# The first stage of a two-block transformer kernel: two channel pairs multiply the un-normalised input, and one product sums the squares

## The chip, the cores and the metric

The kernel runs on one core of a Trainium2 chip. The metric is the time of one execution on the device, in microseconds; of several runs the median is given. The engines of the core run side by side and wait for each other by semaphores: TensorE (PE, with its weight loads PEld), VectorE (DVE), ScalarE (ACT), GpSimd (POOL), and SyncE (SP), which only issues the loads here.

## The reference

Two transformer blocks follow each other on 512 tokens of width 1024, in float32. Only the start of the first one matters here:

```python
def rms_norm(x, g):
    xf = x.astype(jnp.float32)
    y = xf * lax.rsqrt(jnp.mean(xf * xf, axis=-1, keepdims=True) + EPS)
    return (y * g.astype(jnp.float32)).astype(x.dtype)
...
    h = rms_norm(x, norm1_g)
    z = h @ w_in
    q, k, v, xr, yr, gate_logits = jnp.split(z, IN_SPLITS, axis=-1)
...
    rnn = rg_lru(causal_depthwise_conv(xr, conv_w, conv_b), w_rg_a, b_rg_a, w_rg_x, b_rg_x,
                 rg_lambda) * jax.nn.gelu(yr)
```

xr and yr have 1280 columns each. The factor 1/sqrt(mean) depends on the token alone, so it can be applied to a column of `h @ w_in` after the product as well as before it. Attention, merge, an expert layer and the whole second block follow.

## The kernel before

**Tiles.** The activations stand transposed, channels on partitions, 512 tokens in the free dimension: X is eight tiles of 128x512. A weight unit is 128 output columns: 128x1024, that is eight blocks of 128x128 for the eight k. Each float32 operand is cut into a high and a low part, and a product is three matmuls (lines 719 to 721, `triple`). ScalarE makes a weight's high part (line 1277), VectorE its low part (line 1748). `raw` holds five loaded units and `whl` five cut ones.

**Order of the units.** `unit_order()` fixes it: 0 and 1 are w_in 24 and 34 (xr and yr of channel pair 0), 2 and 3 pair 1, 4 and 5 pair 2, 6 and 7 pair 3, then two gate units and small ones. Each engine's program is written out by hand and walks through this list; `weights(name, i)` means: cut (or load) up to NW - 1 = 4 units past this one. An engine works strictly in its program's order, so a cut waits for what is written before it.

**The first stage.** SP loads the parameters, X in four quarters, the constants `cst`, five weight units and the lambdas. ScalarE squares each X[k] into scr[k] and forms the high part of X[k] times its gain, VectorE the low part (`gained`). TensorE first sums the squares over the channels with eight products with a matrix of ones (`sums`, line 754), then multiplies pair 0 with the un-normalised, gained X (`two`). ScalarE turns the sum into the factor r (Ln and Exp, which need a function table), VectorE scales X to H (`norm`: one product, line 1756, and one difference, line 1748, per k), ScalarE makes H's high part in between. Pair 0's products are scaled by r out of PSUM by VectorE in `conv4(0)`: xr into `pad`, yr into ST. From pair 1 on TensorE multiplies H, and ScalarE copies xr from PSUM to `pad`.

**Around the change.** Per pair VectorE runs `conv4` (one product, three chained steps), ScalarE the conv's high part, then gelu of yr, with a function table of its own, and between them stand the cuts of later weights. After pair 1's conv VectorE runs `scalars()`, a chain of some thirty small instructions with two exponentials of ScalarE in it; the low part of unit 7 follows behind it. In names of tiles, `whl` is a cut weight, `pb` PSUM, `S` and `ST` one memory under two types.

Of the kernel before, what the change touches and what calls it, by code (L numbers as in the profile page):

```python
# [491 lines left out]
def build(nc, a, out):  # L492
    with ExitStack() as ctx:
# [119 lines left out]
        gh, gl, first_q = oh, ol, (sum_sq, one_sq)  # L613
        o_root = [scr[8]] * 7 + [scr[7]]
# [100 lines left out]
        def tensor(eng, e):  # L715
# [17 lines left out]
            def two(j, outs, hh, hl, ready, done, tag=None):  # L733

                for k in range(8):
                    if k == 4 and tag:
                        sum_of(tag)
# [8 lines left out]
            def sum_of(tag):  # L746
                q.wait_ge(pool, ("sq", tag))
                e.matmul(bank[7], ones, sum_sq, start=True, stop=True, skip_group_check=True).then_inc(
                    prod.up(("sums", tag)), 1)

            def sums(tag, sq, b, lhs=ones):
                for k, s in enumerate(sq):
                    q.wait_ge(act, ("sq", tag, k))
                    last = e.matmul(b, lhs, s, start=k == 0, stop=k == len(sq) - 1, skip_group_check=True)
                last.then_inc(prod.up(("sums", tag)), 1)
# [30 lines left out]
            def recurrence():  # L786
                q.wait_ge(cst_in, "cst")
                sums("1", scr[0:8], bank[7])
                for c in range(0, 10, 2):
                    for d in (c, c + 1):  # L790
                        i = d % 2
                        if d == 0:
                            j = q.unit("w_in", 24)
                            q.unit("w_in", 34)
                            two(j, (bank[0], bank[2]), gh, gl, [("g", "1", k) for k in range(8)], (("xr", 0), ("yr", 0)))
                            continue
                        if d == 2:
                            q.wait_ge(dve, "xr_scaled")
                        elif d > 2:
# [460 lines left out]
        def scalar(eng, e):  # L1260
            q, hi_done, logs = Waits(eng, units), [0], [False]
# [89 lines left out]
            def recurrence():  # L1351
                q.wait_ge(prm_in, "prm")
                for k in range(8):
                    q.wait_ge(x_in[k // 2], ("x", k // 2))
                    run(ACT.Square, scr[k], X[k]).then_inc(act.up(("sq", "1", k)), 1)
                    e.activation(gh[k], X[k], ACT.Copy, scale=prm("norm1_g", k)).then_inc(act.up(("ghi", "1", k)), 1)
                    if k == 5:
                        split(2)
                norm("1", scr, scr[8], bank[7], Hh, lambda: split(4))
                for c in range(0, 10, 2):  # L1360
                    for d in (c, c + 1):
# [4 lines left out]
                        if d:  # L1366
# [1413 lines left out]
```

## Time and profile before

| | us |
|---|---|
| median of 3 runs | 2969.61 (2969.41 to 2971.81) |
| profiled execution, its own time | 2972.36 |
| span of the profiled execution, first to last instruction | 2970.2 |
| TensorE busy | 2921.5 (98%) |
| VectorE busy | 1906.8 (64%) |
| ScalarE busy | 1152.3 (39%) |
| GpSimd busy | 842.9 (28%) |

The profile shows one execution; its own time is 2.2 us more than its span. Matmuls overlap, so a busy TensorE is not one at its peak. Of the chain that ended last 80% lies on TensorE, 12% on VectorE and 4% on ScalarE, and the first stage is the first 60 to 90 us of it. In the rows further down L719 to L721 are the three matmuls of a product.

### The profile page before, as it was taken

The page shows a single profiled execution, that of the slowest core. Times are in us where ns is not written, and L with a number is a line of the kernel's source. Part 1 is how long each engine was busy: PE and PEld are TensorE (multiplying, and loading weights), DVE is VectorE, ACT ScalarE, POOL GpSimd, SP SyncE. Part 2 cuts the span into 40 slices and gives each one's busy share as a digit, 9 for nine tenths or more (in the row PEclk, how much of TensorE's full clock was granted, in tenths as well). Part 3 has the DMA queues.
Part 4 walks back from the last instruction along what each step waited for, and adds up shares of the span by engine and source line. Part 5 has one row for each costly group of instructions (what it writes and reads, how often), then busy time and mean ns, then how long its engine had stood idle before and what let it go on. Part 6 is the DMA issues. An engine that isn't in the chain of part 4 may idle for free.

```text
span 2970.2 us, 35823 instructions
## 1 busy us (share of the span) xinstructions
PE 2921.5 (98%) x14079; PEld 2509.6 (84%) x14079; DVE 1906.8 (64%) x3255; ACT 1152.3 (39%) x1704; POOL 842.9 (28%) x523
## 2 busy tenths in 40 slices
PE   8999999999999999999999999999999999999999
PEld 6877777789889999999999999998888877788887
DVE  6664665578888895426787788865444567644443
ACT  5674665443333334433323223223222355532221
POOL 0000000228788888872332232321000400210000
PEclk9999999999999999999999999999999999999999
DMA  4325564336656666798988888842332321133222
GB/s 141 112 92 212 199 223 167 132 103 144 136 127 139 153 154 146 166 272 322 333 311 308 287 310 314 318 142 86 99 100 94 122 71 50 51 99 99 93 93 71
DMA packets 240808, 489.29 MB, mean 165 GB/s; under 512 B 97664, under 2 KB 149440, under 8 KB 240128
## 3 DMA queue, kind: packets, MB, share of 16 engines
q1 hardware_dynamic: 175680, 417.87, 42.3%
q0 software_dynamic: 64960, 69.14, 10.3%
q8 instruction: 111, 1.82, 0.2%
q14 instruction: 57, 0.47, 0.0%
HBM read 443.18 MB, written 77.23 MB: 175 GB/s over the span
## 4 chain that ended last, share of the span: by engine, by line
PE 80%; DVE 12%; ACT 4%; issue 3%; POOL 1%; DMA 0%; SPq 0%; POOLq 0%; ACTq 0%
PE pb L719 25%; PE pb L721 25%; PE pb L720 25%; DVE whl L1748 2%; ACT scr L1274 2%; DVE ST L1748 1%; ACT whl L1277 1%; PE pb L1011 1%; DVE ST L1756 1%; DVE S L1748 1%; DVE su L1997 1%; DVE ST L1998 1%; DVE su L2000 1%; DVE scr L1748 1%; PE pb L894 1%
## 5 line engine op out<-in xcount | busy, mean ns | idle before, releaser
L719 PE MATMUL pb<-H,whl 128*128 128x512 f32 (+1 forms) x2400 | 939.7, 392 | 6.4 <-ACT scr L1274 2.3
L721 PE MATMUL pb<-H,whl 128*128 128x512 f32 (+1 forms) x2400 | 911.5, 380 | 0.0
L720 PE MATMUL pb<-H,whl 128*128 128x512 f32 (+1 forms) x2400 | 910.8, 380 | 0.0
L1748 DVE TENSOR_TENSOR whl<-raw,whl 128x1024 fp32r<-128x1024 f32 (+5 forms) x554 | 650.7, 1189 | 256.3 <-ACT whl L1277 219.8
L1277 ACT ACTIVATE whl<-raw 128x1024 fp32r<-128x1024 f32 (+5 forms) x554 | 544.6, 1003 | 361.2 <-PE pb L721 360.1
L719 PE MATMUL pb<-S,whl 128*128 128x448 f32 (+2 forms) x1732 | 654.9, 378 | 14.2 <-DVE S L1748 5.7
L720 PE MATMUL pb<-S,whl 128*128 128x448 f32 (+2 forms) x1732 | 649.6, 375 | 0.0
L721 PE MATMUL pb<-S,whl 128*128 128x448 f32 (+2 forms) x1732 | 649.5, 375 | 0.0
L719 PEld LDWEIGHTS pb<-H,whl 128*128 128x128 f32 x2400 | 451.4, 188 | 83.8 <-issue 8.8
L720 PEld LDWEIGHTS pb<-H,whl 128*128 128x128 f32 x2400 | 451.5, 188 | 72.2 <-issue 6.0
L721 PEld LDWEIGHTS pb<-H,whl 128*128 128x128 f32 x2400 | 450.6, 188 | 71.9
L2400 POOL DMA_INDIRECT gd<-scr,place x256 | 438.2, 1712 | 137.8 <-issue 77.1
L719 PEld LDWEIGHTS pb<-S,whl 128*128 128x128 f32 x1732 | 327.9, 189 | 60.9 <-DVE S L1748 7.2
L720 PEld LDWEIGHTS pb<-S,whl 128*128 128x128 f32 x1732 | 327.8, 189 | 42.6 <-issue 1.2
L721 PEld LDWEIGHTS pb<-S,whl 128*128 128x128 f32 x1732 | 327.6, 189 | 42.5
L2379 POOL TENSOR_TENSOR pad<-X 128x512 f32<-128x512 f32 x32 | 46.2, 1442 | 862.4 <-DVE X L1748 833.3
L1274 ACT ACTIVATE scr<-pb 128x448 f32<-128x448 f32 (+1 forms) x130 | 71.0, 546 | 386.2 <-PE pb L721 364.5
L1748 DVE TENSOR_TENSOR scr<-pb,scr 128x512 f32<-128x512 f32 x96 | 66.0, 691 | 210.7 <-PE pb L721 199.7
L2433 POOL DMA_INDIRECT scr<-in_pv_rows,su x64 | 94.8, 1482 | 232.1 <-DVE scr L1756 204.8
L1277 ACT ACTIVATE S<-GA 128x896 fp32r<-128x896 f32 x60 | 57.2, 953 | 252.6 <-DVE GA L1748 247.0
L2387 POOL DMA_INDIRECT scr<-in_pu_rows,su x64 | 91.8, 1434 | 217.0 <-DVE scr L1756 167.0
L1748 DVE TENSOR_TENSOR X<-X,pb 128x448 f32<-128x448 f32 (+1 forms) x144 | 86.2, 630 | 92.8 <-PE pb L721 78.8
(224 smaller groups left out, 2573.8 us busy)
## 6 DMA issues: line engine op xcount, KB each, us to landing
raw<-in_pu SPq DMA_DIRECT2D x128, 512.0 KB
raw<-in_pv SPq DMA_DIRECT2D x128, 512.0 KB
raw<-in_w_in SPq DMA_DIRECT2D x72, 512.0 KB
ad<-scr SPq DMA_DIRECT2D x128, 224.0 KB
GA<-gd SPq DMA_DIRECT2D x60, 448.0 KB, 4.2
GA<-ad SPq DMA_DIRECT2D x60, 448.0 KB, 5.9
raw<-in_wg SPq DMA_DIRECT2D x44, 512.0 KB
raw<-in_wu SPq DMA_DIRECT2D x44, 512.0 KB
```

Of the source, the lines that this page charges most:

```text
L719: e.matmul(o, lh, h, start=start, stop=False, skip_group_check=True)
L720: e.matmul(o, lh, l, start=False, stop=False, skip_group_check=True)
L721: return e.matmul(o, ll, h, start=False, stop=stop, skip_group_check=True)
L894: e.matmul(b[:, 0:keys], x[r, t], y[r, 0:keys], start=start, stop=False, skip_group_check=True)
L1011: last = e.matmul(bank[gbank[n % 4]][:, c], hot2[n % 4][:, c], hot1[n % 4][:, c], start=True, stop=True, skip_group_check=True)
L1274: return e.activation(o, x, func, **kw)
L1277: return e.activation(o, x, ACT.Copy)
L1748: return e.tensor_tensor(o, x, y, op)
L2379: e.tensor_tensor(one_sq if k else sum_sq, x, x, ALU.mult).then_inc(pool.up(), 1)
L2387: e.indirect_dma_start(urow[j % 3] if j < UROWS else tail_row[j % 4], None, a["pu_rows"], bass.IndirectOffsetOnAxis(ap=expert[:, j:j + 1], ...
L2400: e.indirect_dma_start(g_rows, bass.IndirectOffsetOnAxis(ap=place[:, b, h, k:k + 1], axis=0), TSv[:, b, h, k:k + 1], None, compute_op=ALU. ...
L2433: e.indirect_dma_start(tail_row[j % 4], None, a["pv_rows"], bass.IndirectOffsetOnAxis(ap=expert[:, j:j + 1], axis=0)).then_inc(row_in[j % ...
```

## The change

Pair 1 now multiplies the un-normalised X as pair 0 does, and both of its results are scaled by VectorE. For that the parts of the gained X stand elsewhere (g1h, g1l), so that ST's pieces for yr 0 and 1 stay free. The squares are added on VectorE into scr[0], and TensorE forms one sum product in place of eight, inside pair 1 before its second k (`at_k=1`). ScalarE loads the function table for Ln and Exp as its first instruction. SP loads units 0 and 1 right behind X's first quarter. The cuts of units 0 to 4, the constants' work of VectorE and the scaling of xr 0 are moved in the order.

```diff
@@ -611,6 +611,7 @@
 gh, gl, first_q = oh, ol, (sum_sq, one_sq)
+g1h, g1l = cut(S_t[:, 1024:5120], 8), cut(S_t[:, 6144:10240], 8)
 o_root = [scr[8]] * 7 + [scr[7]]
@@ -730,10 +731,10 @@
-    def two(j, outs, hh, hl, ready, done, tag=None):
+    def two(j, outs, hh, hl, ready, done, tag=None, at_k=4):
...
         for k in range(8):
-            if k == 4 and tag:
+            if k == at_k and tag:
                 sum_of(tag)
@@ -744,15 +745,13 @@
     def sum_of(tag):
-        q.wait_ge(pool, ("sq", tag))
-        e.matmul(bank[7], ones, sum_sq, start=True, stop=True, skip_group_check=True).then_inc(
+        if tag == "1":
+            q.wait_ge(cst_in, "cst")
+            q.wait_ge(dve, "sq_sum")
+        else:
+            q.wait_ge(pool, ("sq", tag))
+        e.matmul(bank[7], ones, scr[0] if tag == "1" else sum_sq, start=True, stop=True, skip_group_check=True).then_inc(
             prod.up(("sums", tag)), 1)
-
-    def sums(tag, sq, b, lhs=ones):
-        for k, s in enumerate(sq):
-            q.wait_ge(act, ("sq", tag, k))
-            last = e.matmul(b, lhs, s, start=k == 0, stop=k == len(sq) - 1, skip_group_check=True)
-        last.then_inc(prod.up(("sums", tag)), 1)
@@ -784,19 +783,18 @@
     def recurrence():
-        q.wait_ge(cst_in, "cst")
-        sums("1", scr[0:8], bank[7])
+        g1 = [("g", "1", k) for k in range(8)]
         for c in range(0, 10, 2):
...
                 i = d % 2
-                if d == 0:
-                    j = q.unit("w_in", 24)
-                    q.unit("w_in", 34)
-                    two(j, (bank[0], bank[2]), gh, gl, [("g", "1", k) for k in range(8)], (("xr", 0), ("yr", 0)))
+                if d < 2:
+                    j = q.unit("w_in", 24 + d)
+                    q.unit("w_in", 34 + d)
+                    two(j, (bank[i], bank[2 + i]), g1h, g1l, g1, (("xr", d), ("yr", d)), "1" if d else None, 1)
                     continue
-                if d == 2:
-                    q.wait_ge(dve, "xr_scaled")
-                elif d > 2:
+                if d < 4:
+                    q.wait_ge(dve, ("xr_scaled", d - 2))
+                else:
                     q.wait_ge(act, ("xr_raw", d - 2))
@@ -1258,7 +1256,8 @@
 def scalar(eng, e):
-    q, hi_done, logs = Waits(eng, units), [0], [False]
+    q, hi_done, logs = Waits(eng, units), [0], [True]
+    e.preload_act_table_set("natural_log_exp_and_others")
@@ -1350,22 +1349,28 @@
         q.wait_ge(prm_in, "prm")
-        for k in range(8):
-            q.wait_ge(x_in[k // 2], ("x", k // 2))
-            run(ACT.Square, scr[k], X[k]).then_inc(act.up(("sq", "1", k)), 1)
-            e.activation(gh[k], X[k], ACT.Copy, scale=prm("norm1_g", k)).then_inc(act.up(("ghi", "1", k)), 1)
+        for k in range(10):
+            if k < 8:
+                q.wait_ge(x_in[k // 2], ("x", k // 2))
+                e.activation(g1h[k], X[k], ACT.Copy, scale=prm("norm1_g", k)).then_inc(act.up(("ghi", "1", k)), 1)
+            if k == 1:
+                split(2)
+            elif k > 1:
+                run(ACT.Square, scr[k - 2], X[k - 2]).then_inc(act.up(("sq", "1", k - 2)), 1)
             if k == 5:
-                split(2)
-        norm("1", scr, scr[8], bank[7], Hh, lambda: split(4))
+                split(3)
+            elif k == 7:
+                split(4)
+        norm("1", scr, scr[8], bank[7], Hh, lambda: split(5))
         for c in range(0, 10, 2):
...
                     weights("w_in", 34)
-                if d:
+                if d > 1:
                     q.wait_ge(prod, ("xr", d))
-                    q.wait_ge(dve, ("conv", d - 2) if d > 1 else ("pad0", i))
+                    q.wait_ge(dve, ("conv", d - 2))
                     copy(pad[i][:, 32:544], bank[i]).then_inc(act.up(("xr_raw", d)), 1)
@@ -1380,11 +1385,11 @@
                     run(ACT.Exp, sq[1], sq[1]).then_inc(act.up("softplus_exp"), 1)
-                if d:
+                if d > 1:
                     q.wait_ge(prod, ("yr", d))
                 else:
-                    q.wait_ge(dve, "yr_scaled")
-                run(ACT.Gelu_apprx_tanh, rlf[d], bank[2 + i] if d else rlf[0]).then_inc(act.up(("gelu", d)), 1)
+                    q.wait_ge(dve, ("yr_scaled", d))
+                run(ACT.Gelu_apprx_tanh, rlf[d], bank[2 + i] if d > 1 else rlf[d]).then_inc(act.up(("gelu", d)), 1)
             if c:
@@ -1770,9 +1775,10 @@
-    def norm(tag, xs, gains, sq, r, hi, lo, mid=lambda: None):
+    def norm(tag, xs, gains, sq, r, hi, lo, mid=lambda: None, between=lambda k: None):
         mid()
         for k in range(9):
+            between(k)
             if k < 8:
@@ -1810,15 +1816,20 @@
+    def scaled_x(c):
+        q.wait_ge(prod, ("xr", c))
+        tt(pad[c][:, 32:544], bank[c], scr[8], ALU.mult).then_inc(dve.up(("xr_scaled", c)), 1)
+
     def conv4(c, beside=()):
         i, cv, w = c % 2, rhf[c], [prm("conv_w", 4 * c + j) for j in range(4)]
-        if c:
+        if c > 1:
             q.wait_ge(act, ("xr_raw", c))
         else:
-            q.wait_ge(prod, ("xr", 0))
-            then(tt(pad[0][:, 32:544], bank[0], scr[8], ALU.mult), "xr_scaled")
-            q.wait_ge(prod, ("yr", 0))
-            tt(rlf[0], bank[2], scr[8], ALU.mult).then_inc(dve.up("yr_scaled"), 1)
+            if c:
+                scaled_x(1)
+            q.wait_ge(prod, ("yr", c))
+            tt(rlf[c], bank[2 + c], scr[8], ALU.mult).then_inc(dve.up(("yr_scaled", c)), 1)
+            q.wait_ge(dve, dve.n)
         then(ts(cv, pad[i][:, 32:544], w[3], ALU.mult, prm("conv_b", c), ALU.add))
@@ -1853,10 +1864,17 @@
         q.wait_ge(prm_in, "prm")
-        for k in range(8):
-            gained("1", k, "norm1_g", gh, gl, ("g", "1", k))
-            if k == 5:
+        for k in range(10):
+            if k < 8:
+                gained("1", k, "norm1_g", g1h, g1l, ("g", "1", k))
+            if k == 1:
                 split(2)
+            elif k == 8:
+                split(4)
+            if k > 2:
+                q.wait_ge(act, ("sq", "1", k - 2))
+                then(tt(scr[0], scr[0], scr[k - 2], ALU.add), *(["sq_sum"] if k == 9 else []))
+        norm("1", X, gains("norm1_g"), scr, scr[8], Hh, Hl, between=lambda k: scaled_x(0) if k == 2 else split(5) if k == 4 else None)
         q.wait_ge(cst_in, "cst")
@@ -1865,7 +1883,6 @@
             e.memset(pad[i][:, 0:32], 0.0).then_inc(dve.up(("pad0", i)), 1)
-        norm("1", X, gains("norm1_g"), scr, scr[8], Hh, Hl, lambda: split(4))
         for c in range(0, 10, 2):
@@ -2455,8 +2472,8 @@
-    def load_x(name):
-        for i in range(4):
+    def load_x(name, quarters=range(4)):
+        for i in quarters:
             e.dma_start(X_t[:, 1024 * i:1024 * i + 1024].rearrange("p (k t) -> p k t", k=2),
@@ -2472,7 +2489,9 @@
         e.dma_start(prm_t[:, :], a["prm"]).then_inc(prm_in.up("prm"), 16)
-        load_x("x")
+        load_x("x", (0,))
+        load(2)
+        load_x("x", (1, 2, 3))
         e.dma_start(cst_t[:, :], a["cst"]).then_inc(cst_in.up("cst"), 16)
@@ -2490,6 +2509,7 @@
         q.wait_ge(dve, ("h", "1", 7))
+        q.wait_ge(dve, ("yr_scaled", 1))
         q.wait_ge(dve, "lambda_sums")
...
         load_gate(1, 9, 1)

```

What stands on TensorE at its start before (scr are the squares, L754 the sum products, then pair 0):

```order
L754 MATMUL pb<-scr,cst 128x512 [waits act_results,constants_landed]
L754 MATMUL pb<-scr,cst 128x512 [waits act_results] x7
L719 MATMUL pb<-S,whl 128x512 [waits weight_low_parts,dve_results]
L720 MATMUL pb<-S,whl 128x512
L721 MATMUL pb<-S,whl 128x512
L719 MATMUL pb<-S,whl 128x512 [waits weight_low_parts]
L720 MATMUL pb<-S,whl 128x512
```

TensorE with the change, from the end of pair 0 to the second k of pair 1 (L753 is the sum product):

```order
L720 MATMUL pb<-S,whl 128x512
L721 MATMUL pb<-S,whl 128x512
L722 MATMUL pb<-S,whl 128x512
L720 MATMUL pb<-S,whl 128x512 [waits weight_low_parts]
L721 MATMUL pb<-S,whl 128x512
L722 MATMUL pb<-S,whl 128x512
L720 MATMUL pb<-S,whl 128x512 [waits weight_low_parts]
L721 MATMUL pb<-S,whl 128x512
L722 MATMUL pb<-S,whl 128x512
L753 MATMUL pb<-scr,cst 128x512 [waits dve_results,constants_landed]
L720 MATMUL pb<-S,whl 128x512
L721 MATMUL pb<-S,whl 128x512
```

The eight sum products ahead of pair 0 are gone; one stands behind all of pair 0 and the first k of pair 1.

VectorE before, at the end of the norm and the start of pair 0's conv (unit 4's low part, the two scalings, the conv):

```order
L1756 SCALAR_TENSOR_TENSOR scr<-X,prm,scr 128x512
L1748 TENSOR_TENSOR H<-scr,H 128x512 [waits act_results] x2
L1748 TENSOR_TENSOR whl<-raw,whl 128x1024 [waits weight_high_parts]
L1748 TENSOR_TENSOR pad<-pb,scr 128x512 [waits pe_products]
L1748 TENSOR_TENSOR ST<-pb,scr 128x512 [waits pe_products,dve_results]
L1753 TENSOR_SCALAR ST<-pad,prm 128x512
L1756 SCALAR_TENSOR_TENSOR ST<-pad,prm,ST 128x512 [waits dve_results] x3
```

VectorE with the change, from the norm's first product on:

```order
L1761 SCALAR_TENSOR_TENSOR scr<-X,prm,scr 128x512 [waits act_results,dve_results]
L1761 SCALAR_TENSOR_TENSOR scr<-X,prm,scr 128x512
L1753 TENSOR_TENSOR H<-scr,H 128x512 [waits act_results]
L1753 TENSOR_TENSOR pad<-pb,scr 128x512 [waits pe_products]
L1761 SCALAR_TENSOR_TENSOR scr<-X,prm,scr 128x512
L1753 TENSOR_TENSOR H<-scr,H 128x512 [waits act_results]
L1761 SCALAR_TENSOR_TENSOR scr<-X,prm,scr 128x512
L1753 TENSOR_TENSOR H<-scr,H 128x512 [waits act_results]
L1753 TENSOR_TENSOR whl<-raw,whl 128x1024 [waits weight_high_parts]
L1761 SCALAR_TENSOR_TENSOR scr<-X,prm,scr 128x512
```

The scaling of xr 0 and the low part of unit 4, which stood behind the norm, now stand within it, ahead of its third and fifth product.

ScalarE from H's high parts to the high part of unit 5 (the `whl<-raw` of weights_landed0), before:

```order
L1277 ACTIVATE H<-scr 128x512 [waits dve_results] x8
L1277 ACTIVATE whl<-raw 128x1024 [waits weights_landed4]
L1277 ACTIVATE S<-ST 128x512 [waits dve_results]
L1274 ACT_TABLE_LOAD
L1274 ACTIVATE ST<-ST 128x512
L1277 ACTIVATE whl<-raw 128x1024 [waits pe_products,weights_landed0]
L1277 ACTIVATE pad<-pb 128x512 [waits pe_products]
```

ScalarE with the change, from the high part of unit 4 to that of unit 5:

```order
L1276 ACTIVATE whl<-raw 128x1024 [waits weights_landed4]
L1273 ACTIVATE scr<-pb,cst 128x512 [waits pe_products]
L1273 ACTIVATE scr<-scr 128x512 [waits act_results]
L1276 ACTIVATE H<-scr 128x512 [waits dve_results] x8
L1276 ACTIVATE S<-ST 128x512 [waits dve_results]
L1273 ACT_TABLE_LOAD
L1273 ACTIVATE ST<-ST 128x512
L1276 ACTIVATE whl<-raw 128x1024 [waits weights_landed0]
```

Unit 4 now stands ahead of the norm, unit 5 as before behind the conv's high part, the table load and gelu(0), and the copy to `pad` is gone.

## Rows read from the trace of the kernel before

**Rows 1.** The chain that ended last, its start: start us, us, what.
```profile
3.07 7.91 DMA cst<-in_cst
11.02 10.04 PE pb L754 x16
21.08 1.28 ACT L1267
...
40.59 1.28 ACT L1274
...
42.52 0.96 ACT whl L1277
...
58.62 1.14 DVE whl L1748
```

**Rows 2.** Timeline of TensorE: start us, us, engine line op, operands, xcount, [idle before <-releaser].
```profile
20.49 0.79 PE L719 MATMUL pb<-S,whl 128*128 128x512 f32 x1
...
31.81 0.39 PE L719 MATMUL pb<-H,whl 128*128 128x512 f32 x1
...
59.89 0.47 PE L719 MATMUL pb<-H,whl 128*128 128x512 f32 x1 [0.71 <-DVE whl L1748]
```

**Rows 3.** Busy us (xcount) by stretch: stretch, length, PE, PEld, DVE, ACT, POOL, PEclk, DMA share, GB/s.
```profile
60.00:147.00 87.00, 87.00 (x383) 71.77 (x384) 57.67 (x75) 57.50 (x80) 0.00 (x0) 1.00 0.35 117
...
2573.50:2580.30 6.80, 5.15 (x12) 4.09 (x13) 2.97 (x5) 3.58 (x6) 2.38 (x3) 0.50 0.00 0
177.30:180.70 3.40, 3.22 (x8) 2.58 (x9) 1.36 (x3) 3.37 (x6) 0.00 (x0) 0.50 0.51 104
```

**Rows 4.** Timeline of TensorE's weight loads in the eight sum products.
```profile
15.45 0.34 PEld L754 LDWEIGHTS pb<-scr,cst 128*128 128x128 f32 x1 [0.52 <-issue]
16.31 0.34 PEld L754 LDWEIGHTS pb<-scr,cst 128*128 128x128 f32 x1 [0.52 <-issue]
17.03 0.19 PEld L754 LDWEIGHTS pb<-scr,cst 128*128 128x128 f32 x1 [0.38 <-ACT S L1356]
17.46 0.19 PEld L754 LDWEIGHTS pb<-scr,cst 128*128 128x128 f32 x1 [0.24 <-issue]
```

**Rows 5.** DMA issues of 1.1 to 1.5 us, of 1.5 to 2.0, and SP's timeline: us to landing last.
```profile
X<-in_x SPq DMA_DIRECT2D x1, 512.0 KB, 4.2
...
X<-in_x SPq DMA_DIRECT2D x2, 512.0 KB, 4.8
...
1.18 1.84 SPq L2460 DMA_DIRECT2D X<-in_x  x4
```

**Rows 6.** Timeline of ScalarE, high parts.
```profile
7.25 0.71 ACT L1356 ACTIVATE S<-X,prm 128x512 fp32r<-128x512 f32 x1
...
13.52 1.99 ACT L1277 ACTIVATE whl<-raw 128x1024 fp32r<-128x1024 f32 x2
...
17.68 1.99 ACT L1277 ACTIVATE whl<-raw 128x1024 fp32r<-128x1024 f32 x2
```

**Rows 7.** Timeline of VectorE, first stage.
```profile
8.08 0.75 DVE L1756 SCALAR_TENSOR_TENSOR S<-X,prm,S 128x512 fp32r<-128x512 f32 x1 [8.08 <-ACT S L1356]
...
18.48 0.29 DVE L1752 TENSOR_SCALAR prm<-prm 128x1 f32<-128x1 f32 x3
...
19.19 2.32 DVE L1748 TENSOR_TENSOR whl<-raw,whl 128x1024 fp32r<-128x1024 f32 x2
...
32.80 1.48 DVE L1748 TENSOR_TENSOR H<-scr,H 128x512 fp32r<-128x512 f32 x2
...
36.40 0.69 DVE L1748 TENSOR_TENSOR ST<-pb,scr 128x512 f32<-128x512 f32 x1
...
43.50 1.22 DVE L1748 TENSOR_TENSOR whl<-raw,whl 128x1024 fp32r<-128x1024 f32 x1 [2.20 <-ACT whl L1277]
```

**Rows 8.** Timeline of TensorE at two later idle times.
```profile
177.48 0.77 PE L719 MATMUL pb<-S,whl 128*128 128x512 f32 x1 [2.85 <-DVE whl L1748]
...
2575.15 0.80 PE L719 MATMUL pb<-S,whl 128*128 128x512 f32 x1 [2.03 <-DVE S L1748]
```

## What I predict, and from what

> **What bounds the kernel now.** I read first the chain that ended last, from its start, because the change touches only the first stage. It runs [rows 1]: SP issues the loads, the constants `cst` come down (3.07 + 7.91 = 10.98 us), TensorE does the eight sum products from 11.02 for 10.04 us, ScalarE loads a function table at 21.08, the norm follows, and then the chain does *not* go over TensorE. It goes over VectorE and ScalarE: a table load and gelu(0) (40.59 to 42.52), the high part of a weight (42.52), two convolutions, the small chain `scalars()`, and the low part of weight unit 7 (58.62 + 1.14 = 59.76). Only at 59.89 does TensorE take the chain over, after 0.71 us idle [rows 2]. From there it has no idle time up to 147 us [rows 3]. So TensorE's products between 20.49 and 59.2 us are not on the path: what counts is **when the low part of unit 7 is ready**, because whatever shifts it shifts the rest. Units are numbered as they are consumed: 0 and 1 are pair 0 (w_in 24, 34), 2 and 3 are pair 1, 4 and 5 channel pair 2, 6 and 7 channel pair 3.
>
> The second thing to see is TensorE's clock. In the weight loads of the sum products the starts are 0.86 us apart at 15.45 and 16.31, 0.72 at 17.03 and 0.43 at 17.46 [rows 4]. The same operation runs at half rate (1.2 GHz) first and then at full rate (2.4 GHz). The page's granted clock prints 1.00 for all of it, so the pitch decides. A product of the triple takes (31.81 - 20.49) / 48 = 0.236 us at full rate [rows 2].
>
> **Loads.** X's first quarter lands at 1.18 + 4.2 = 5.4 us. The median of the first two is 4.8, so the second, issued 0.46 later, took 5.4 and landed near 7.05; cst, three slots on, landed at 11.0, so a slot takes some 1.4 us [rows 1, 5]. The weights behind it had landed when ScalarE came for them (13.52 and 17.68, without idle time) [rows 6]. The new order keeps the bytes and swaps slots: units 0 and 1 land near 7.05 and 8.5, X's other quarters near 9.7, 11.0 and 12.3, cst near 13.5, units 2 to 4 near 14.8, 16.2 and 17.5.
>
> **Start of the products.** ScalarE's high part takes 1.0 us (two in 1.99) and the high part of one 512-column piece of the gained X 0.71 [rows 6]; VectorE's low part of a weight takes 1.2 [rows 7]. Unit 0: 7.05 + 1.0 + 0.1 + 1.2 = 9.4, so the first product starts near 9.5 instead of 20.49. The table now loads under the wait for X and costs nothing there.
>
> TensorE comes out of idleness, and now the products pay for it, not the sum products. In the trace half rate lasted from 11.02 to between 16.31 and 17.03, that is some 5.8 us [rows 1, 4]. The same length from 9.5 costs 2.9 us. Pair 0 ends at 9.5 + 48 x 0.236 + 2.9 = 23.7. VectorE feeds it: each k needs one 0.75 us piece (8.08) and one add, priced as the 0.69 us of the same shape at 36.40 [rows 7], about 1.45; k = 7 is ready near 19.0, needed near 22. The adds end near 23.4, because the low parts of units 2 and 3 stand between them. Neither is late.
>
> **The sum.** It now stands behind 54 products (at_k = 1 of pair 1). TensorE gets to it at 23.7 + 1.4 = 25.1; two passes at 0.43 and 0.56 from the last issue to the end (20.49 to 21.06 before) make 26.5 [rows 1, 2]. That is **+5.4 us**. Seven sum products are gone, worth 8.8 us on TensorE, but the one left waits behind 15.
>
> **From the sum to unit 7**, by the same rows:
> - the table load of 1.28 at 21.08 is gone [rows 1]: **-1.3**.
> - in the norm VectorE never idles; the change puts scaled_x(0) (0.6) and the low part of unit 4 (1.15) between, takes 34.28 to 36.40 (that low part and the pad scaling, 2.1) away behind h(7), and puts the constants' work of 18.48 to 19.19 (0.7) there instead [rows 7]: 0.6 + 1.15 - 2.1 + 0.7 = **+0.35**.
> - conv 1 started as soon as unit 5's low part (43.50) was through, from a `pad` that ScalarE had copied [rows 7]. Now VectorE scales both banks itself first, 0.6 + 0.7, not hidden since ScalarE waits for this conv: **+1.2**.
> - gelu(0), its table load, and the `scalars()` chain stay as they are: 0.
>
> Sum: 5.4 - 1.3 + 0.35 + 1.2 = **+5.6**. Unit 7 is ready at 59.76 + 5.6 = 65.4, unit 6 near 56.0, unit 5 at 44.72 + 4.4 = 49.1 (the 1.2 comes after it).
>
> **What TensorE does meanwhile.** Pair 1 ends at 23.7 + 11.3 + 0.9 = 35.9 (before: 42.7, so 6.8 ahead). xr(2) uses H, whose last part comes near 39.9, just in time, and ends at 41.5. There unit 5 is missing, because its high part is queued on ScalarE behind the conv and gelu(0), and TensorE stands until 49.2. The lead is gone here: before, yr(2) began at 20.49 + 5 x 5.5 = 48. It idles again for some 2.5 to 3.5 us before unit 7.
>
> **The clock after a wait.** Idle times of 2.85 and 2.03 us in the trace each came with a stretch at clock 0.50, 3.4 and 6.8 us long [rows 3, 8], while 0.71 us before 59.89 did not [rows 2, 3]. The first of these stretches holds eight products in 3.2 us [rows 3]. That costs 1.7 us, or up to 3.4 when it starts in the idle time and lasts. The same is to be expected at 41.5, where it is covered by the next wait, and before unit 7, where nothing covers it, since TensorE is the chain from there: **+1.7**, bounds 0 and 2.9.
>
> Total **+7.2**. The profiled execution would be 2972.36 + 7.2 = 2979.6 (span 2970.2 + 7.2); it was 2.7 above the median of the runs, so the forecast is 2969.6 + 7.2 = **2976.8 us**.
>
> The Trainium skill ("TensorE: Matmul & The Clock Gate", Part 1, on the clock gate) says that where the first rise falls differs from run to run of one kernel and warns against fitting it to a count. The one trace can't show that. [...]
>
> **Bounds of the uncertain terms.** First half-rate stretch: 0 to 3.4 us of loss instead of 2.9 (so -2.9 to +0.5). Second: 0 to 2.9 instead of 1.7. The order of the landings: a slot more or less, -0.3 to +1.4. VectorE's adds are 1.7 us ahead of TensorE; if they take 0.3 us more each (each waits for the one before it to be complete; the two differences from 32.80 take 1.48), they become the last to come and add up to 0.5.
>
> **Rivals.**
> 1. *No clock loss at the second wait, or an early first rise* (within 0.2%). The shift is 5.6, or 7.2 - 2.9 = 4.3: 2974 to 2975.2. For it: two of the terms depend on when the clock changes. Against: the trace's idle times of this size come with the fall.
> 2. *Faster.* If unit 5 and 7 were not late, TensorE's 6.8 us lead at 35.9 would go through to the end: 2969.6 - 6.8 = 2962.8. It decides at 41.5 us: unit 5's low part must be ready by then, and by 52.4 unit 7's. For it: the products do start 11 us earlier and TensorE is busy throughout the trace from 20.49 on. Against: the chain of the trace doesn't touch those products, and ScalarE's row order has unit 5 behind gelu(0). A part of it could be true if the sum came far earlier than 26.5, but it can't issue before 9.5 + 54 x 0.236 = 22.2.
> 3. *The adds or the loads come late* (slower still). If cst or units 2 and 3 land a slot or two late, or the adds pass 25.1 us, everything moves on: +9 to +11, 2979 to 2981.
> 4. *The change does not do what it says*: the order shows that it does; no chance of its own.
>
> **How the numbers follow.** A difference under 0.2% (5.9 us) is about what a measurement of this kernel can't tell from none. Forecast (shift over 5.9 to 9): 0.51, its own range 2975.6 to 2978.7. Rival 1: 0.34. Rival 2: 0.07, with part of a gain (under 0.2%) counted in rival 1. Rival 3: 0.08. So slower 0.51 + 0.08 = 0.59, same 0.34, faster 0.07. The range 2972.0 to 2980.0 leaves out rival 2, the small end of rival 1 and most of rival 3.
>
> **What would show it.** In the profile after: first product near 9.5 us; one sum product, ending near 26.5; VectorE's first norm product near 27.9; TensorE idle about 7.5 us from 41.5, releaser the low part of a weight; again 2 to 4 us ending near 65.4; then no idle time; a clock of 0.50 for some us after each. Wrong would be: no idle time over 2 us between 35 and 66 (rival 2), the sum's end before 23 us (rise early), or a clock of 1.00 right after 65.4 (rival 1).

## The result, and the profile after

| | before | after |
|---|---|---|
| median of 14 runs each, us | 2971.02 (2969.06 to 2973.25) | 2977.96 (2974.39 to 2980.67) |
| profiled execution, span, us | 2970.2 | 2972.6 |
| TensorE busy, us | 2921.5 | 2915.5 |

The changed kernel is slower. Its median is 6.9 us above that of before; the ratio of the two is put at 1.0020, with an interval of 1.0013 to 1.0027, that is 5.9 us (3.9 to 8.0). The forecast was 7.2 us more than before, 2976.8 against a measured 2977.96. The profiled execution of after took 2974.39 us, the shortest of its fourteen.

**The chain that ended last, after** (start us, us, what), to hold beside [rows 1]:

```profile
8.95 0.76 PE pb L720
...
22.98 0.87 PE pb L753 x2
...
42.50 1.28 ACT L1273
...
44.42 0.95 ACT whl L1276
...
52.42 1.23 DVE whl L1753
...
61.83 1.14 DVE whl L1753
```

TensorE is on it at the start, in the first 54 products (8.95 to 22.98) and the one sum product (0.87 us). Then the chain goes over VectorE and ScalarE as before, through the table load of gelu(0) (42.50) and the cuts of units 5, 6 and 7, to the low part of unit 7 at 61.83 + 1.14 = 62.97 (58.62 + 1.14 before).

**TensorE's timeline, after**, to hold beside [rows 2]: its first product, the sum product, and the two waits for a low part:

```profile
8.95 0.76 PE L720 MATMUL pb<-S,whl 128*128 128x512 f32 x1 [8.95 <-DVE whl L1753]
...
22.81 1.02 PE L753 MATMUL pb<-scr,cst 128*128 128x512 f32 x2
...
46.77 0.76 PE L720 MATMUL pb<-H,whl 128*128 128x512 f32 x1 [7.93 <-DVE whl L1753]
...
63.11 0.54 PE L720 MATMUL pb<-H,whl 128*128 128x512 f32 x1 [3.63 <-DVE whl L1753]
```

The first product came 11.5 us earlier (8.95 against 20.49) and pair 1 was done 9.5 us earlier (the next unit starts at 33.24 against 42.69), and all of that was waited away before unit 5 (7.93 us) and again before unit 7 (3.63 us). Unit 7 is used 3.22 us later than before (63.11 against 59.89). Behind it stands what [rows 3] shows of other idle times, a stretch at half rate:

```profile
9.00:12.20 3.20, 3.20 (x8) 2.32 (x9) 3.05 (x4) 3.09 (x6) 0.00 (x0) 1.00 1.01 411
12.20:22.80 10.60, 10.60 (x48) 8.77 (x47) 9.22 (x13) 7.82 (x12) 0.00 (x0) 1.00 0.77 301
...
46.70:49.70 3.00, 2.93 (x7) 2.38 (x8) 2.89 (x5) 0.00 (x0) 0.00 (x0) 0.50 0.15 44
...
63.30:66.80 3.50, 3.50 (x9) 2.71 (x9) 2.70 (x5) 0.99 (x2) 0.00 (x0) 0.51 0.40 150
66.80:150.00 83.20, 83.20 (x368) 68.86 (x367) 54.41 (x70) 55.45 (x78) 0.00 (x0) 1.00 0.35 110
```

These are stretches of after in the columns of [rows 3], PEclk third from the end. In 9:12.2 the page prints 1.00, but eight products in 3.2 us are the half-rate pitch; 48 follow in 10.6. At 46.7 and at 63.3 the clock reads 0.50 (1.2 GHz), at 66.8 it is back at 1.00 (2.4 GHz), and TensorE has no idle time up to 150.

**A mark inside the execution.** TensorE's products behind unit 7 are the same in every kernel here, and one idle time of 2.85 us recurs among them, at 177.48 before [rows 8]. After:

```profile
182.09 0.47 PE L720 MATMUL pb<-S,whl 128*128 128x512 f32 x1 [2.85 <-DVE whl L1753]
```

The part behind this mark takes 2792.7 us before and 2790.5 after, and between 2789 and 2799 in all twelve profiles of this study, with no order that follows the first stage. (The part is the span less the start of the mark.) A profile of one execution therefore says more at the mark than at its end: here + 4.61 us at the mark, + 2.4 at the end.

### The profile page after: what moved, and what is told of

Read it like the earlier page. It is cut to its first block, busy times and chain, and to the rows that moved or that the text cites. A ratio compares the mean times of both kernels' runs of the same rounds, so it can differ in the third digit from the quotient of the medians.

```text
span 2972.6 us, 35808 instructions
## 1 busy us (share of the span) xinstructions
PE 2915.5 (98%) x14065; PEld 2508.2 (84%) x14065; DVE 1913.0 (64%) x3264; ACT 1151.1 (39%) x1702; POOL 844.0 (28%) x523
## 4 chain that ended last, share of the span: by engine, by line
PE 78%; DVE 12%; ACT 4%; POOL 3%; issue 2%; DMA 1%; SPq 0%; POOLq 0%; ACTq 0%; DVEq 0%
PE pb L720 25%; PE pb L722 25%; PE pb L721 25%; DVE whl L1753 2%; POOL gd L2417 2%; ACT scr L1273 1%; ACT whl L1276 1%; DVE su L2014 1%; DVE ST L2015 1%; DVE ST L1753 1%; DVE su L2017 1%; DVE S L1753 1%; DVE ST L1761 1%; PE pb L1009 1%; DVE scr L1753 1%
## 5 line engine op out<-in xcount | busy, mean ns | idle before, releaser
L720 PEld LDWEIGHTS pb<-S,whl 128*128 128x128 f32 x1748 | 330.2, 189 | 70.6 <-issue 11.1
```

The costliest lines, as they stand in the source:

```text
L720: e.matmul(o, lh, h, start=start, stop=False, skip_group_check=True)
```

## The experiments

Each is an edit of one of the two kernels. Runs of one comparison shared a chip; medians of different comparisons are not set against each other, ratios to before are.

### The changed kernel again

> The changed kernel, unchanged, a second time beside the others. Theory (unit 7's readiness plus a half-rate stretch sets the time): 5 to 9 us slower than before. The first product's start (8.95 us in the first profile), the first half-rate stretch (3.2 us there) and the two idle times (7.9 and 3.6 us) are fixed by the program except for the half-rate stretches, which should differ by up to 3 us between executions; that would be the spread of its runs. Rival (nothing varies at the start): the start of the product with unit 7 is at 63.1 us again to within 0.2 us.

Measured: 1.0020 times before (1.0011 to 1.0029). The same rows of TensorE's timeline, the mark last:

```profile
9.21 0.77 PE L720 MATMUL pb<-S,whl 128*128 128x512 f32 x1 [9.21 <-DVE whl L1753]
...
23.89 1.02 PE L753 MATMUL pb<-scr,cst 128*128 128x512 f32 x2
...
47.84 0.77 PE L720 MATMUL pb<-H,whl 128*128 128x512 f32 x1 [7.93 <-DVE whl L1753]
...
64.16 0.47 PE L720 MATMUL pb<-H,whl 128*128 128x512 f32 x1 [3.46 <-DVE whl L1753]
...
183.14 0.47 PE L720 MATMUL pb<-S,whl 128*128 128x512 f32 x1 [2.85 <-DVE whl L1753]
```

The program is the same and so are its two idle times (7.93 and 7.93, 3.63 and 3.46), but the sum product stands at 23.89 in place of 22.81 and unit 7 at 64.16 in place of 63.11. The first product was 0.26 us later, because X's first quarter landed later (ScalarE's first piece starts at 5.53 against 5.20); the rest is the clock: in the nine profiles of kernels that begin with products, the half-rate pitch lasted between 3.2 and 6.3 us. So the rival, that the start is fixed to 0.2 us, fell. The Trainium skill ("TensorE: Matmul & The Clock Gate", Part 1, on the clock gate) says that this point differs from run to run of one kernel; these traces agree (3.2 and 4.7 us in two executions of one program).

### The cut of unit 7 ahead of scalars()

```diff
                         if d == 1:
+                            split(8)
                             scalars()
```

(and the same line on ScalarE ahead of its two exponentials)

> The changed kernel with one more cut of weights (unit 7) written ahead of scalars() on ScalarE and VectorE. Theory: unit 7 is then ready near 55 us, before TensorE wants it at 59.4, so the idle time of 3.6 us before it and the half-rate stretch behind it (1.7 us) go: 5 us less than the changed kernel, so within 0.1% of before. Rival A (the 7.9 us at 38.8 are what costs): about no difference to the changed kernel. Rival B (VectorE is simply 1.2 us later with everything else, scalars() is needed): the idle time comes back before unit 8.

Measured: 1.0022 (1.0013 to 1.0031), no gain. TensorE's timeline:

```profile
47.98 0.76 PE L720 MATMUL pb<-H,whl 128*128 128x512 f32 x1 [7.92 <-DVE whl L1754]
...
61.20 0.50 PE L720 MATMUL pb<-H,whl 128*128 128x512 f32 x1 [0.25 <-ACT ST L1273]
...
69.92 0.80 PE L720 MATMUL pb<-H,whl 128*128 128x512 f32 x1 [2.97 <-DVE whl L1754]
```

The first wait is there as before (7.92), unit 7 no longer waits for its low part, but 2.97 us of idle time stand at 69.92, before unit 8, whose cut is still behind scalars(), with a half-rate stretch behind them: unit 8 takes 8.3 us (69.92 to 78.22) where a unit at full rate takes 5.44. I had expected 5 us less; the rival B of this run is what happened. One cut taken past a chain of 8 us moves the wait by one unit.

### Products into the idle time before unit 7

```diff
+                        if d == 3:
+                            for k in range(5):
+                                triple(bank[5], Hh[k][:, 0:128], Hl[k][:, 0:128], Hh[k], Hl[k], True, True)
                         linear(q.unit("w_in", 34 + d), bank[2 + i], Hh, Hl, h1, ("yr", d))
```

> The changed kernel with 15 added products on TensorE (H with itself into a bank that nobody reads) between xr(3) and yr(3), some 3.4 us of work in the idle time before unit 7. Nothing else is moved. Theory: unit 7 is used at the same time (63.1 in the first profile), but TensorE's clock stays at 1.00 behind it, so the run is 1.7 us (1 to 2.9) faster than the changed kernel. Rival (the idle time alone costs, the clock does not matter): 0 to 0.3 us slower than the changed kernel.

Measured: 1.0011 (1.0002 to 1.0020), median 2976.78 beside 2978.51 of the changed kernel on the same chip, so 1.7 us less; the intervals of the two ratios overlap. Its timeline, with the first of the added products (no `whl` among its operands), unit 7's first and the mark:

```profile
62.05 0.39 PE L720 MATMUL pb<-H 128*128 128x512 f32 x1
...
65.45 0.39 PE L720 MATMUL pb<-H,whl 128*128 128x512 f32 x1
...
182.86 0.49 PE L720 MATMUL pb<-S,whl 128*128 128x512 f32 x1 [2.86 <-DVE whl L1756]
```

And the stretch of 58 to 66 us, in the columns of [rows 3], without a gap and at clock 1.00:

```profile
58.00:66.00 8.00, 8.00 (x37) 6.64 (x36) 6.75 (x31) 3.57 (x6) 0.00 (x0) 1.00 0.00 1
```

The medians alone would not settle it. From the start of unit 7's product to the mark it takes 182.86 - 65.45 = 117.41 us here, 118.98 in both profiles of the changed kernel (182.09 - 63.11, 183.14 - 64.16) and 117.59 before (177.48 - 59.89). Work that computes nothing made this part of the kernel 1.6 us shorter (1.4 if one takes off the 0.15 us by which it delayed unit 7, counted from the sum product): the half-rate stretch is a cost of its own. Its full size shows against the three kernels below in which TensorE does not wait for unit 7 at all: they take 117.24 or 117.25 us to the mark, 1.7 less. The kernel before, with its short wait, itself paid 0.3 of that.

### The cuts moved forward

```diff
-                norm("1", scr, scr[8], bank[7], Hh, lambda: split(5))
+                norm("1", scr, scr[8], bank[7], Hh, lambda: split(7))
+                split(8)
...
-                norm("1", X, gains("norm1_g"), scr, scr[8], Hh, Hl, between=lambda k: scaled_x(0) if k == 2 else split(5) if k == 4 else None)
+                split(7)
+                norm("1", X, gains("norm1_g"), scr, scr[8], Hh, Hl, between=lambda k: scaled_x(0) if k == 2 else None)
+                split(8)
...
                         if d == 1:
+                            split(10)
                             scalars()
...
-                        if d > 1:
+                        if d > 3:
                             q.wait_ge(act, ("gelu", d - 2))
+                        else:
+                            q.wait_ge(dve, ("yr_scaled", d - 2))
```

(The first hunk and a second `split(10)` are ScalarE's, the next two VectorE's, the last TensorE's; in the file they stand in another order.)

> The changed kernel with the cuts moved: units 5 and 6 ahead of the norm (in VectorE's 2.9 us of idle time at 22.5), unit 7 right behind the norm, units 8 and 9 ahead of scalars(); and TensorE's yr(2) and yr(3) wait for the scaling of yr(0) and yr(1) out of PSUM, not for gelu. Theory (TensorE's lead was lost only to late cuts): no idle time over 1 us between 35 and 67 us, unit 7 used near 51 us in place of 63.1, the first gate unit near 56 in place of 65.5 before; 7 to 10 us faster than before, 13 to 17 faster than the changed kernel. Rival (VectorE's chain as a whole, scalars() in it, is the bound of the stage): the idle time only moves to a later unit, and the time is that of before within 2 us.

Measured: 0.9991 (0.9982 to 1.0000), median 2969.11 beside 2972.56, where 7 to 10 us of gain were expected. Its sum product and TensorE's two waits in the timeline:

```profile
23.99 1.10 PE L753 MATMUL pb<-scr,cst 128*128 128x512 f32 x2 [0.32 <-DVE scr L1757]
...
41.23 0.50 PE L720 MATMUL pb<-H,whl 128*128 128x512 f32 x1 [1.14 <-DVE ST L1757]
...
73.15 0.76 PE L720 MATMUL pb<-S,whl 128*128 128x512 f32 x1 [4.39 <-ACT scr L1275]
```

Two stretches of it, in the columns of [rows 3]:

```profile
41.30:68.70 27.40, 27.40 (x120) 22.37 (x120) 21.55 (x55) 10.78 (x15) 0.00 (x0) 1.00 0.15 57
69.00:78.00 9.00, 4.85 (x12) 3.88 (x13) 4.84 (x7) 8.66 (x13) 0.00 (x0) 0.62 0.61 177
```

The 7.93 us are gone: 27.4 us of products without a gap behind 41.3, and unit 7 is used at 52.28 (near 51 expected, 59.89 before). But where before had no wait at all, one of 4.39 us ends at 73.15, for a sigmoid of ScalarE, with a mean clock of 0.62 about it. ScalarE is late because the conv of pair 2 stands behind scalars() on VectorE (the next run tests this), and gelu and the sigmoid behind that conv. The run bundles three things, the cuts, their places on both engines and TensorE's wait for the scaling in place of gelu; "Unit 5 cut in the norm" below shows why a cut alone does not do it. So half of my theory fell: late cuts lost the lead first, scalars() would have lost most of it anyway.

### The cuts moved forward, and scalars() moved to pair 3

```diff
                         if d == 1:
                             split(10)
+                        if d == 3:
                             scalars()
```

(on top of the last edit, and the exponentials on ScalarE likewise)

> The kernel with the early cuts (e4) and scalars(), with its two exponentials on ScalarE, moved from pair 1 to pair 3. In e4 TensorE ran from 41.2 to 68.8 us without idle time and then waited 4.4 us for a sigmoid of ScalarE, which the chain leads back to scalars(); behind it stood a half-rate stretch of 6.8 us (3.4 lost). Theory (scalars() is the last thing on the path of this stage): the wait and the stretch go, so 7 to 8 us less than e4 and 9 to 12 less than before, some 2961. Rival (the sum of VectorE's work bounds the stage): the wait comes back within 10 us behind, and the time stays within 2 us of e4.

Measured: **0.9973 (0.9962 to 0.9984)**, median 2968.17 beside 2975.72 on that chip: 7.6 us faster than before, and so, by the two ratios to before, some 14 faster than the changed kernel. That is less than the 9 to 12 expected. The rival wanted the time within 2 us of the last run; the mark is 5.4 us earlier (171.01 against 176.37). The 7 to 8 expected there took the whole stretch of 6.8 us at half rate as running time, 3.4 lost, but it began at 71.0, inside the idle time, and TensorE ran only from 73.15 to 77.8 in it, which costs 2.3. So 4.4 + 2.3 less the 1.6 us of the wait that is left make 5.1.

TensorE's timeline, the mark last:

```profile
9.37 0.77 PE L720 MATMUL pb<-S,whl 128*128 128x512 f32 x1 [9.37 <-DVE whl L1758]
...
40.71 0.50 PE L720 MATMUL pb<-H,whl 128*128 128x512 f32 x1 [0.36 <-DVE ST L1758]
...
69.83 0.47 PE L720 MATMUL pb<-S,whl 128*128 128x512 f32 x1 [1.62 <-ACT scr L1275]
...
171.01 0.47 PE L720 MATMUL pb<-S,whl 128*128 128x512 f32 x1 [2.85 <-DVE whl L1758]
```

The stretch behind it, in the columns of [rows 3]:

```profile
70.00:150.00 80.00, 80.00 (x353) 66.03 (x353) 54.47 (x71) 58.84 (x82) 0.00 (x0) 1.00 0.36 117
```

The waits are down to 0.36 and 1.62 us, neither with a half-rate stretch behind it, and the mark is at 171.01, 6.5 us ahead of before and 11.1 ahead of the changed kernel. The two pairs' early products pay once nothing on the other two engines is late for what follows. The same moves without the early products could not give this: before, TensorE has no idle time from 20.49 to the mark but the one ahead of unit 7, and the run "Two single edits of the kernel before" below finds 1.2 us to be had there.

### scalars() alone moved to pair 3

```diff
-                        if d == 1:
+                        if d == 3:
                             scalars()
```

(an edit of the changed kernel, the exponentials on ScalarE likewise)

> The changed kernel with nothing but scalars() (and its exponentials) moved from pair 1 to pair 3; units 5 and 6 stay late. Theory: the idle time of 7.9 us before unit 5 stays, the one of 3.6 before unit 7 goes and none replaces it (unit 8's cut no longer stands behind scalars()), with its half-rate stretch of 1.7 us: 5 us less than the changed kernel, within 0.1% of before. Rival (the 7.9 us set the time alone, with the lead): no difference to the changed kernel.

Measured: 0.9994 (0.9985 to 1.0003) beside 1.0020 of the changed kernel in its two comparisons.

TensorE's timeline:

```profile
48.09 0.77 PE L720 MATMUL pb<-H,whl 128*128 128x512 f32 x1 [7.93 <-DVE whl L1753]
...
61.06 0.39 PE L720 MATMUL pb<-H,whl 128*128 128x512 f32 x1
...
178.30 0.48 PE L720 MATMUL pb<-S,whl 128*128 128x512 f32 x1 [2.84 <-DVE whl L1753]
```

The stretch behind it, in the columns of [rows 3]:

```profile
58.00:150.00 92.00, 92.00 (x408) 76.17 (x407) 62.42 (x106) 62.32 (x87) 0.00 (x0) 1.00 0.36 114
```

As expected: the wait of 7.93 us before unit 5 is untouched, none follows it, and the kernel is level with before. Unit 5 is used at 48.09, before at 48.13: the idle time of 7.9 us on its own is no loss against before, it is the lead given back. The half-rate stretch behind it is one: with it unit 5 takes 7.5 us (to 55.62) in place of 5.44. Here nothing covers those 2.1 us; the missing wait before unit 7 gives 1.2 of them back, and the mark is 0.8 us later than before (178.30 against 177.48). In the changed kernel the wait before unit 7 covers them. What made the change slower than before is unit 7. From unit 7 to the mark it is 178.30 - 61.06 = 117.24 us.

### Unit 5 cut in the norm

```diff
-                norm("1", scr, scr[8], bank[7], Hh, lambda: split(5))
+                norm("1", scr, scr[8], bank[7], Hh, lambda: split(6))
```

(and `split(6)` for `split(5)` in VectorE's norm)

> The changed kernel with the cut of unit 5 moved into the norm, nothing else. Theory (each wait is covered by the next): TensorE still waits at 39 us, now some 6.7 us for gelu(0), and unit 7 is used only some 2.2 us earlier than 63.1 to 64.2, near 61.5, since the high and low part leave the chain between gelu(0) and the second conv but 1.1 us come back in the norm. Rival (unit 5 alone is late): no idle time at 39 us, and unit 7 used 7 us earlier, near 56.

TensorE's timeline:

```profile
46.89 0.80 PE L720 MATMUL pb<-H,whl 128*128 128x512 f32 x1 [5.88 <-ACT ST L1273]
...
62.07 0.47 PE L720 MATMUL pb<-H,whl 128*128 128x512 f32 x1 [1.94 <-DVE whl L1753]
```

One execution, 2975.45 us beside 2975.72: the wait before unit 5 is 5.88 us in place of 7.93 (6.7 expected), and now ends with gelu (`ACT ST`), not with a low part. Unit 7 is used at 62.07; the sum product of this execution stood at 24.04, so the sound comparison is with the repeat (23.89 and 64.16): 2.1 to 2.2 us earlier, as expected. The idle time of 1.94 us before it left no half-rate stretch: from there to its mark (179.61) it takes 117.54 us, as much as before (117.59), 0.3 more than where there is no wait.

### The loads in the old order

```diff
-                load_x("x", (0,))
-                load(2)
-                load_x("x", (1, 2, 3))
+                load_x("x")
```

> The changed kernel with SP's load order of before (all of X, then cst, then the weights). Theory: unit 0 lands near 12.3 in place of 6.5 us, the first product starts near 15, and since the sum product stands behind 54 products everything after it moves with that: sum product near 28 to 29, unit 7 used near 68 to 69, that is 4 to 6 us more than the changed kernel. Rival (the sum is bound by the squares and adds on VectorE, which do not need the weights early): sum product near 24, unit 7 as in the changed kernel.

TensorE's timeline:

```profile
14.80 0.77 PE L720 MATMUL pb<-S,whl 128*128 128x512 f32 x1 [14.80 <-DVE whl L1753]
...
29.63 1.02 PE L753 MATMUL pb<-scr,cst 128*128 128x512 f32 x2
...
69.90 0.47 PE L720 MATMUL pb<-H,whl 128*128 128x512 f32 x1 [3.24 <-DVE whl L1753]
```

One execution, 2989.12 us beside 2975.72; its part behind the mark is the longest of the twelve (2798.4 us), so only the stage is read. The first product starts at 14.80, 5.6 to 5.9 us later than in the changed kernel, the sum product at 29.63, 5.7 to 6.8 later, and unit 7 at 69.90, 5.7 to 6.8 later (4 to 6 expected). The sum does hang on the products ahead of it, one for one, and VectorE's adds are not what it waits for here: they end at 27.33, 2.3 us before it. (They too are later than in the changed kernel, since ScalarE cuts units 0 and 1 ahead of the second quarter of X.)

### Two single edits of the kernel before

With scalars() moved to pair 3:

> The kernel before with nothing but scalars() (and its exponentials) moved from pair 1 to pair 3. Theory (before, TensorE was only 0.7 us ahead of unit 7, so its products were nearly the bound themselves): the idle time of 0.71 us before 59.89 goes, unit 7's product starts near 59.2, and the idle time of 2.85 us that ends at 177.48 ends near 176.8; 0.7 us in all. Rival (the cuts and scalars() are the bound of the stage): unit 7 is ready 8 us earlier and so is everything: the idle time ends near 170.

TensorE's sum products and the mark:

```profile
11.26 9.50 PE L754 MATMUL pb<-scr,cst 128*128 128x512 f32 x16 [11.26 <-DMA cst<-in_cst]
...
175.94 0.47 PE L719 MATMUL pb<-S,whl 128*128 128x512 f32 x1 [2.85 <-DVE whl L1748]
```

With the function table loaded first:

> The kernel before with nothing but the function table for Ln and Exp loaded as ScalarE's first instruction. Both table loads of the first 22 us (at 5.42 and at 21.08) go. Theory: the norm starts 1.28 us earlier than 23.76, unit 7 is ready near 58.5, and TensorE, whose products of the stage end at 59.2, gains only its 0.7 us of idle time; the idle time that ends at 177.48 ends near 176.8. Rival (the whole 1.28 us reaches the end): it ends near 176.2.

TensorE's sum products, its first other product and the mark:

```profile
11.34 8.65 PE L754 MATMUL pb<-scr,cst 128*128 128x512 f32 x16 [11.34 <-DMA cst<-in_cst]
19.43 0.79 PE L719 MATMUL pb<-S,whl 128*128 128x512 f32 x1
...
175.18 0.77 PE L719 MATMUL pb<-S,whl 128*128 128x512 f32 x1 [2.85 <-DVE whl L1749]
```

One execution each, 2971.23 and 2966.67 beside 2972.67. The mark moved by 1.5 and 2.3 us where I expected 0.7, and not by the 7.5 us of the first run's rival. Part is the clock at the start, which was back at full rate earlier in both: the sum products took 9.50 and 8.65 us against 10.04. With the table first, pair 0 started at 19.43 against 20.49, so 1.06 of its 2.3 us; with scalars() later it started at 20.19, 0.30 of 1.5. The rest, 1.24 us in both, is the wait before unit 7, which neither has. The page's idle time of 0.71 us understates it: the starts at 58.78 and 59.89 are 1.11 us apart where 0.23 is the pitch, 0.9 us. The other 0.3 lies right behind it: units 7 and 8 took 5.60 and 5.62 us before (starts at 59.89, 65.49 and 71.11) and 5.43 to 5.44 in both edits, so that from unit 7 to the mark it is 117.25 us in both (175.94 - 58.69, 175.18 - 57.93) against 117.59. What makes those two units slower behind a short wait is not shown. That before was close to bound by its products holds: removing either item from the other two engines gives 1.2 us, as there is no other wait to take away. For the table that number alone does not tell the expectation from its rival, which had 1.28 reach the end; that the wait is gone, with unit 7's low part ready at 57.4 and TensorE there at 57.93, does.

## Why the prediction was right

The direction and the mechanism held. The size held to about a microsecond; that 7.2 lies within 0.3 us of the medians' 6.9 is luck.

- **What bounds the stage** (unit 7's low part, not TensorE's products): right. In every kernel in which unit 5 or 7 stayed late the lead was lost; with all cuts early the time came level with before or just under it, and with scalars() out of the way too it fell clearly below.
- **Loads and first product**: unit 0 was cut at 6.49 and unit 1 at 7.87 in ScalarE's timeline of after:

```profile
6.49 1.06 ACT L1276 ACTIVATE whl<-raw 128x1024 fp32r<-128x1024 f32 x1
7.87 1.06 ACT L1276 ACTIVATE whl<-raw 128x1024 fp32r<-128x1024 f32 x1 [0.33 <-DMA raw<-in_w_in]
```

  I had 7.05 and 8.5 for their landings, and 9.5 for the first product; 8.95 to 9.79 was measured in the eight profiles of this load order.
- **The first half-rate stretch**: 5.8 us taken, 3.2 and 4.7 measured in the changed kernel, 3.2 to 6.3 over all. This term was mis-sized: in the profiled execution it cost 1.6 us and not 2.9, in the nine on average 2.4.
- **The sum**: ready at 22.98 + 0.87 = 23.85, 24.9 in the repeat; predicted 26.5. The +5.4 of the forecast was +2.8 here and +3.85 in the repeat. Of the 2.65 us too many in the first, 1.3 are the clock, 0.55 the start, 0.5 that I took 0.236 us for each of 54 products, a mean over a piece with a slow first product, where 0.227 is the pitch, and 0.4 a slip in the sum: 25.1 + 0.43 + 0.56 is 26.1, and 26.5 counts one pass twice (1.02 measured for the two).
- **VectorE in time**: its adds ended at 21.05 + 1.41 = 22.46, half a microsecond before TensorE came for the sum, not 1.7. With the clock up early the adds can become the bound: in "The cuts moved forward", the same up to there, TensorE waited 0.32 us for them (the line at 23.99).

  In VectorE's timeline of after, the last adds, the last of h and the scaling of yr 0:

```profile
21.05 1.41 DVE L1753 TENSOR_TENSOR scr<-scr 128x512 f32<-128x512 f32 x2
...
36.11 1.47 DVE L1753 TENSOR_TENSOR H<-scr,H 128x512 fp32r<-128x512 f32 x2
...
38.22 0.66 DVE L1753 TENSOR_TENSOR ST<-pb,scr 128x512 f32<-128x512 f32 x1
```

- **From the sum to unit 7**: predicted 65.4 - 26.5 = 38.9, measured 62.97 - 23.85 = 39.1. h(7) at 36.11 + 1.47, the constants' work, the scaling at 38.22: step by step as worked out. The -1.3, +0.35 and +1.2 stand, with -1.2, +0.3 and +1.3 measured (sum to the norm's first product 1.48 us against 2.70; from there to the conv 13.58 against 13.25; between the low parts of units 5 and 7 16.34 against 15.02).
- **What TensorE does meanwhile**: pair 1 was 9.5 us ahead at its end, not 6.8, and unit 5 was wanted at 38.7, not 41.5; the sum came earlier too, so the waits came out right: 7.5 and 2.5 to 3.5 predicted, 7.93 and 3.46 to 3.63 measured.
- **The clock behind the last wait**: 1.7 predicted. It is 1.7 against the kernels that do not wait there (118.98 against 117.25), but before paid 0.3 for its own short wait, so 1.4 of it is difference.

The shift of unit 7 was 3.2 and 4.3 us in the two profiles, where I predicted 5.5 to 5.6; with the clock's 1.4 the mark moved 4.6 and 5.7, against 7.2. The medians moved 6.9 and 6.0. The microsecond or two between mark and median is what single profiles leave open: they are draws of a start that varies, and the profile of after is an early one. Its sum product, at 22.81, is the earliest of the eight profiles of this load order, whose mean is 24.03; and before, pair 0 started at 20.49 in the one profile, at 20.19 and 19.43 in its two edits. An estimate for a typical start is then 4.6 + 1.2 + 0.4 = 6.2 us, which fits both medians, and the 7.2 were a microsecond too many. That the forecast met the measured 6.9 to 0.3 us, inside an interval of 4 us, is luck; and the median of before in this comparison was itself 1.4 higher than the one that the forecast was set on.

Rival 1 (within 0.2%) was near: of its two conditions one was half met, the rise came earlier than taken (1.6 to 3.1 us lost in the nine profiles, 2.9 taken), and the other was not, the stretch behind unit 7 came. The ratio of 1.0020 lies on its border. Rival 2 (the lead goes through) failed at the point named: unit 5 was wanted near 38.7 us and its low part ended at 46.6. What I had not seen is how little a single cut would have helped.

## What to carry to other kernels

Work moved off a busy engine's start is only worth what the other engines are early for: list, for each of the next units, when its operand is ready, and move the latest one. A serial chain of small instructions (here 8 us) in front of a cut is paid by every engine that needs the cut; put it where its own result is first needed. And compare single profiles at a mark that recurs in both: the part behind it spread over 9 us here, enough to hide a difference of 5 us at the end.

## What the runs showed of the hardware

- The length of the half-rate stretch at the start differed between two executions of one program, 3.2 and 4.7 us; with 0.26 us of a later start it moved the sum product by 1.08 us.
- An idle time of TensorE of 3.5 to 3.6 us cost a further 1.7 us behind it (118.98 against 117.25 us to the mark), and products that nobody reads took all but 0.2 of that away. One of 1.94 us left no such stretch, one of 2.03 before did [rows 3, 8].
- The length of the idle time does not decide it alone. In after and in the repeat, two executions of one program, the same one of 1.79 us stands in TensorE's timeline (after's first, the repeat's second):

```profile
536.71 0.50 PE L720 MATMUL pb<-S,whl 128*128 128x512 f32 x1 [1.79 <-DVE scr L1753]
...
537.73 0.50 PE L720 MATMUL pb<-S,whl 128*128 128x512 f32 x1 [1.79 <-DVE scr L1753]
```

  Behind the first the granted clock is 0.50 from 538 to 541 us, with eight products in 3.0 us; behind the second it stays at 1.00 from 537.8 to 545, with 32 in 7.2 us. And of the twelve idle times of 2.85 us at the mark, eleven had a stretch at half rate behind them and one, in "The loads in the old order", none.
- The page's granted clock prints 1.00 from the span's start, while the pitch of the products shows half rate for the first microseconds; only the pitch tells it there.
